# Eight gather slots in place of nine, and the page table loaded at the start of the last stage

## The reference

```python
hp = rmsnorm(xp, norm_mix)
b_g, c_g, x_in, q_lat, kv_lat, kr_raw, gate_c, gate_a = in_projection(hp, w_in)
attn = prompt_attention(...)          # causal, 8 heads; new tokens: sample_attention(...)
xp = xp + branch_merge(...)           # convolution branch and attention branch
xp = xp + peer(rmsnorm(xp, norm_ffn), ...)

def one_seq(args):                    # new tokens: keys come from pages of the cache
    pages, sqn, sqr, sckv, skr = args
    ckv_all = jnp.concatenate([pool_ckv[pages].reshape(-1, KV_LORA), sckv], axis=0)
    ...

def peer_block(h, w_peer_q, sub_keys, expert_u, expert_v):   # 8 heads, the best 16 of 16384 experts each
    ...
    a = jax.nn.gelu(jnp.einsum('thkd,td->thk', expert_u[eidx], h), approximate=False)
    return jnp.einsum('thk,thkd->td', g * a, expert_v[eidx])
```

## Time and profile before

| | us |
|---|---|
| median of 3 runs | 3808.12 (3807.24 to 3813.5) |
| the profiled execution: its own time | 3808.12 |
| its span in the profile | 3806.3 |
| first and last gather issued at | 639.9 and 3780.8 |
| PE, DVE, ACT, POOL busy | 3145.2, 2626.9, 1359.3, 1102.3 |
| DMA moved | 1289.23 MB, of it 1107.36 MB by the gathers |

### The profile page before, as it was taken

How to read it: one execution, slowest core, us unless ns; L and a number is a source line. 1 busy time by engine, 2 the same in 40 slices (tenths; PEclk the granted TensorE clock), 3 DMA queues, 4 the chain that set the end, 5 groups by cost and what they waited for, 6 DMA issues and landing times.

```text
span 3806.3 us, 35282 instructions
## 1 busy us (share of the span) xinstructions
PE 3145.2 (83%) x10224; PEld 1773.7 (47%) x10224; DVE 2626.9 (69%) x5829; ACT 1359.3 (36%) x3982; POOL 1102.3 (29%) x1252
## 2 busy tenths in 40 slices
PE   6797898858899999467878898899488988888877
PEld 4433686524555555134444454445144544566421
DVE  1355114987677789877677867789777677756874
ACT  1222202338712233255563222343244444212333
POOL 0000001343333333333333333334233333322342
PEclk9898699978899999788889999999699989766999
DMA  2112255999999998799999999999799899999999
GB/s 91 38 37 64 76 154 188 403 366 396 389 415 418 405 373 344 280 403 403 398 415 420 419 419 420 410 407 403 289 417 390 342 395 386 385 392 419 409 387 381
DMA packets 234016, 1289.23 MB, mean 339 GB/s; under 512 B 45467, under 2 KB 59867, under 8 KB 98340
## 3 DMA queue, kind: packets, MB, share of 16 engines
q0 software_dynamic: 152064, 1107.36, 71.6%
q1 hardware_dynamic: 80036, 175.28, 13.1%
q10 hardware_dynamic: 1728, 4.39, 0.3%
HBM read 1273.53 MB, written 13.40 MB: 338 GB/s over the span
## 4 chain that ended last, share of the span: by engine, by line
PE 30%; DMA 27%; DVE 21%; ACT 6%; issue 5%; POOL 2%; SPq 0%; DVEq 0%; POOLq 0%; ACTq 0%
DMA tl_uv<-in_uv,tl_idx 24%; PE tl_y L926 9%; DVE tl_uv L1501 7%; PE tl_f L1175 7%; DVE tl_acc L1482 4%; PE tl_f L1155 3%; PE tl_f L1203 2%; PE tl_f L1186 2%; PE tl_f L987 2%; PE tl_f L1099 1%; POOL tl_uv L857 1%; DMA w_tail<-in_w_merge 1%; PE tl_f L1051 1%; DMA w_tail<-in_w_conv 1%; DVE tl_eq L1601 1%
## 5 line engine op out<-in xcount | busy, mean ns | idle before, releaser
L1501 DVE CUSTOM_DVE_ANT_0 tl_uv<-tl_uv,tl_h 128x1024 f32<-128x1024 f32 x1056 | 1269.5, 1216 | 471.0 <-DMA tl_uv<-in_uv,tl_idx 460.6
L857 POOL DMA_INDIRECT tl_uv<-in_uv,tl_idx x1056 | 1043.8, 988 | 1770.8 <-PE tl_y L926 1071.5
L926 PE MATMUL tl_y<-tl_uv,tl_diag 128*128 128x512 f32 (+1 forms) x2428 | 1285.7, 672 | 292.9 <-ACT tl_diag L1222 292.2
L926 PEld LDWEIGHTS tl_y<-tl_uv,tl_diag 128*128 128x128 f32 (+1 forms) x2428 | 479.3, 209 | 931.5 <-issue 466.4
L1250 ACT ACTIVATE tl_ge<-tl_a 128x1 f32<-128x1 f32 x1056 | 210.1, 199 | 1230.8 <-DVE tl_a L1501 1229.0
L1482 DVE SCALAR_TENSOR_TENSOR tl_acc<-tl_uv,tl_w,tl_acc 128x1024 f32<-128x1024 f32 x441 | 565.1, 1281 | 65.2 <-ACT tl_w L1234 65.0
L1234 ACT ACTIVATE tl_w<-tl_ge,tl_weight 128x1 f32<-128x1 f32 x1024 | 301.5, 294 | 33.4
L1175 PE MATMUL tl_f<-H,w_tail 128*128 128x384 f32 (+2 forms) x1024 | 271.6, 424 | 13.5 <-DMA w_tail<-in_w_merge 11.9
L869 POOL TENSOR_TENSOR tl_cand<-tl_tv 128x48 f32<-128x48 f32 (+5 forms) x128 | 39.5, 337 | 823.5 <-DVE tl_ti L1533 623.5
L1203 PE MATMUL tl_f<-H,w_tail 128*128 128x384 f32 (+2 forms) x1024 | 262.6, 412 | 6.4 <-DVE H L1803 6.4
L1222 ACT ACTIVATE tl_diag<-K,tl_w 128x128 f32<-128x128 f32 (+1 forms) x607 | 241.2, 397 | 38.7 <-PE tl_y L926 19.6
(11 more groups left out here) (227 smaller groups left out, 3084.7 us busy)
## 6 DMA issues: line engine op xcount, KB each, us to landing
w_tail<-in_w_merge SPq DMA_DIRECT2D x96, 512.0 KB, 7.9
w_tail<-in_w_peer SPq DMA_DIRECT2D x64, 576.0 KB, 7.9
w_tail<-in_w_conv SPq DMA_DIRECT2D x48, 512.0 KB, 7.9
tl_uv<-in_uv,tl_idx POOLq DMA_INDIRECT x1056, 12.5
w_tail<-in_w_mix SPq DMA_DIRECT2D x32, 512.0 KB, 7.9
X<-in_cache SPq DMA_DIRECT2D x48, 128.0 KB
X<-in_x SPq DMA_DIRECT2D x8, 536.0 KB, 6.7
o_y<-tl_acc ACTq DMA_DIRECT2D x8, 512.0 KB, 6.2
```

The costliest lines, as they stand in the source:

```text
L857: pool.indirect_dma_start(UV[:, u % RING, :], None, d["uv"], bass.IndirectOffsetOnAxis(ap=which, axis=0)).then_inc(landed[u % RING], 16)
L926: mm = pe.matmul(Y[0:m, half * 512:(half + 1) * 512], DG[:, (pe_count[u] - 1) % DIAGS, 0:m], UV[:, u % RING, D + half * 512:D + (half + 1) ...
L1501: dve.tensor_tensor_reduce(UV[:, u % RING, 0:D], UV[:, u % RING, 0:D], HP[:], 1.0, 0.0, ALU.mult, ALU.add, A[:, t % 2, i:i + 1]).then_inc( ...
```

## The change

The ring has 8 slots in place of 9. That frees 8192 bytes of each partition. The page table moves from the overlaid region to a place of its own (256 bytes), and its load moves from `decode_loads` to the start of `tail_stage`. The wait for it (`tbl_in`) stays where it was, before the first page. The block that stands for the overlaid region gets 16 numbers (64 bytes) more. In the built program `tl_uv` begins at byte 136160 of a partition, 136096 before, and the tensors behind the ring come 8128 bytes lower, or 7872 bytes behind the page table.

```diff
-RING, WRING, DIAGS = 9, 3, 4
+RING, WRING, DIAGS = 8, 3, 4
...
-            PTB = sb("pages", [1, NSEQ * NPG], I32, c=decoding)
...
-        sb("shared", [P, (2 * CT + KD) * NMAX + 48])
+        sb("shared", [P, (2 * CT + KD) * NMAX + 64])
...
         ACC = sb("acc", [P, D])
+        PTB = sb("pages", [1, NSEQ * NPG], I32)
...
                 sp.dma_start(KRS[:], d["s_kr"]).then_inc(dec_in, 16)
-                sp.dma_start(PTB[:], d["pages"]).then_inc(tbl_in, 16)
                 sp.wait_ge(tbl_in, 16)
...
             sp.dma_start(STATE[:], d["state"]).then_inc(conv_in, 16)
+            sp.dma_start(PTB[:], d["pages"]).then_inc(tbl_in, 16)
```

## The result

| | before | after |
|---|---|---|
| median, us | 3810.81 (3807.24 to 3813.53, 4 runs) | 3855.88 (3852.59 to 3856.81, 4 runs) |
| the profiled execution: its own time | 3808.12 | 3849.86 |
| mean granted TensorE clock in it, as a share of 2.4 GHz (the lower level, 1.2, is 0.5) | 0.884 | 0.874 |

The two medians are 45 us apart. The ratio, estimated with further runs of the changed kernel, is 1.0108, with a 95% interval of [1.0092, 1.0125]: about 41 us slower. Measured once more in a later session it was 1.0101 [1.0082, 1.0120], 39 us. The forecast was 3826 us, +17.6, and its range ended at 3847, +39. The direction was right and the size was not.

What follows compares the result with a forecast made beforehand. It took the DMA engines' time at work (ceiling 420 GB/s, 2.50 us a gather) and time run dry as the bound. Slot 25.7, table -8.4, its load at the start +0.3: +17.6 on 3808.1, so 3826 us, range 3811 to 3847.

Steps and rivals of the forecast that it cites:

- The slot before and at the entry: Up to and with the entry of decode, the lost slot costs 10.0 + 7.5 + 2.5 = 20.0 us.
- the price of a dry stretch: Where DMA engines run dry, they do so one gather earlier and restart at the same release: 2.50 us; four before decode, 10.0.
- one new dry stretch in each: In three stretches before decode with fastest landings under 7.9 us, one newly dry stretch each: 7.5 us, between 0 and 20.
- The +2.5 us for the entry itself: At the entry of decode the ring fills one gather sooner and one less stands ready after it: +2.5 us.
- The slot behind the entry: Ten dry stretches behind the entry of decode, 2.5 us each, weighted 0.23 by DVE's waits for data: 5.7 us, between 0 and 25.
- Addresses: The ring 64 bytes higher and the tensors behind it lower, with the same engines, shapes and steps: 0.
- The table's load: At the entry of decode, page-number reads and page loads start 8.4 us earlier: -8.4 us, -8.1 with +0.3 at the start.
- A ninth of the ring: Rival: in stretches held by slots each unit takes 9/8 of its time, the upper ends hold: +49.4, 3857.5 us; chance 0.18.
- The table brings little: Rival: the last page loads land among gathers, so 2.4 us are gained in place of 8.4: 3832 us; chance 0.08.
- Eight are enough: Rival: dry stretches are made up for later, the slot costs nothing, the table's gain is left: 3800.0 us; chance 0.06.
- the two nearly cancel: Rival: only the four dry stretches and the entry pay for the slot, 12.5 - 8.1 = +4.4: 3812.5 us; chance 0.14.
- three signs of being wrong: Stretch up to 2700 us takes no longer, PE's wait for pages stays above 30 us, or full windows fall below 415 GB/s.

Runs made afterwards that it cites:

- ring8_only: Before with eight ring slots in place of nine, table's load and shared block as before: ratio 1.0084 [1.0066, 1.0103] to before.
- hold8_all: Before with nine slots at their places, but each gather waits for the release of the unit eight before it, whole span: ratio 1.0096 to before.
- shift_only: Before with the shared block 64 bytes larger, so the ring and all behind it lie 64 bytes higher: ratio 1.0021, again 1.0017, to before.
- hold8_early: Before with nine slots, but gathers below unit 720 (through the entry of decode) wait for the release of the unit eight before: ratio 1.0069 to before.
- ring8_table_first: The changed kernel without the 64 bytes more in the shared block (eight slots, table loaded at the start): ratio 1.0084 [1.0064, 1.0105] to before.
- ring7: The changed kernel with seven ring slots: ratio 1.0270 [1.0256, 1.0284] to before, 3918.7 us.

## Why the prediction was wrong

The sum of parts as measured: the slot 32 to 37 us (ring8_only, hold8_all), the place 6 to 8 (shift_only twice), the table -5.7 with eight slots (from the trace). That is 32 to 39, against the measured 39 to 41. The forecast had 25.7, 0 and -8.1. So of the miss of some 22 us about 9 are the slot's, 7 the place's, 3 the table's, and the rest is within the intervals.

*The slot before and at the entry: 20.0 forecast, 26 [18, 35] measured.* The failed step is the price of a dry stretch, that the DMA engines run dry one gather earlier "and start again at the same release: 2.50 us more", together with "I count one new dry stretch in each". The release does not stay where it was. In the second tile DVE waits 24 us longer for gathers, PE 10.5 us longer for DVE, and PE's products take 5 us more at a lower granted clock, so the slots come back later: at 1140.5 us in place of 1134.0 in the stretch that was followed above. The stretches at 1030 and 1443 us grew by 1 to 2 us and the one at 1595 not at all, less than the price. New ones opened at three places of the second tile alone and cost 3.0 to 4.8 us each. That tile is 16 us longer, and the sum had at most four prices in it, 10 us.

I took one gather for each of three minima, and allowed eight at most. The medians of 9.9 and 9.2 said that half of the gathers there had fewer than two others ahead. In before's trace 50 of the gathers issued up to 2700 us land within the 7.9 us of my test, 20 of them before 1450 us. That the price is convex (34, then 63 us) agrees: each slot taken uncovers gathers which the last one still covered.

The +2.5 us for the entry itself isn't seen there. The first gather behind it goes out 30.5 us after the load of `tl_kr` in before, and 27.9, 29.2 and 28.4 us after it in ring8_only, hold8_early and hold8_all: the ring of eight shortened the entry, since the table's load was through sooner. So the 26 us arise ahead of the entry.

The sum's lower end for the slot, 2.5 us, also leaves out the four dry stretches, for which no lower bound was given; with them it is 12.5.

*The slot behind the entry: 5.7 forecast, 10 [4, 16] measured.* The weight of 0.23 was mis-sized, though its interval holds the forecast. DVE's wait for data is a poor gauge. In the changed kernel it is 18.3 us for 151 products in the same window (compare), 3 us more, while the time grew by 10:

```profile
L1501 DVE CUSTOM_DVE_ANT_0 tl_uv<-tl_uv,tl_h x151: 1197/1212/1223, 2899.8 to 3349.6; 128x1024 f32<-128x1024 f32 x151
...
  DMA tl_uv<-in_uv,tl_idx: 18.3, 17
```

*Addresses: 0 forecast, 6 to 8 us measured.* This step failed as a whole: a term was put at nothing. "The same engines, shapes and steps" left out that the gathers' rate depends on where the ring begins, and the ceiling that the whole sum leant on was one of this place. I divided by 420 GB/s and never asked why it was 420. The rule of the Trainium skill that fits stands on the same page, DMA: Bandwidth & Descriptors, that the prediction drew on for other things.

*The table's load: -8.1 forecast, -8.4 [-13, -3] measured alone.* The mechanism and the size were right for nine slots. With eight, the removed wait had already shrunk from 8.4 us (2726.88 to 2735.3) to 5.7 (2757.28 to 2763.0, where the first read of ring8_only starts), so its removal was worth 5.7; PE's wait for the pages says the same, 30.0 us in ring8_only and 24.5 in ring8_table_first. I priced each edit against before and added, where one edit had made the other smaller: an error of 2.7 us. How much of the 5.7 reaches the end is not shown: ring8_only and ring8_table_first have the same ratio, and with intervals of 0.2% each way that can't tell 0 from 5.7.

*The load at the start, +0.3*, is too small to be told.

*The rivals.* "A ninth of the ring", 3857.5, has the time nearest to the result, but by three causes together and not by its own: the price of the slot is 34 us and not its 57.5. "The table brings little" was right in part, by another way than it said: the page loads did not land late, PE waits 24.6 us. "Eight are enough" and "the two nearly cancel" fell with the slot's 32 to 37 us. None of the three signs of being wrong appeared: the stretch up to 2700 us takes longer, PE's wait is 24.6 us and the full windows are at 419. They tested whether the terms were there, not their size.

*What stays open.* Some 4 us between the middles of the sum of parts (36) and of the whole (40) lie within the intervals. How much of the slot's price passes through PE's clock is not separated from the waits. The mean granted clock fell with the depth, from 0.879 over before's 23 runs to 0.875 in ring8_only's and 0.869 in ring7's, and PE is busy for 3180.5 us in the changed kernel's trace against 3145.2. In the second tile this part is 5 of 16 us; a run that holds the clock and shortens the ring is missing. The chain from DVE's waits to PE's was followed in the second tile alone.

## What to carry to other kernels

Ask of a measured ceiling what it depends on: here the begin of the gathers' buffer, a multiple of 256 or not, was worth 0.6 to 0.8% of the kernel, and a change of some buffer's size moves every buffer behind it. Price the loss of a queue's depth by how many transfers have little ahead of them (the median landing against the least) and by who waits behind each late one, not by one transfer's time for each stretch that is already dry. And price edits together where one changes the queue that the other one waits in.

## What the runs showed of the hardware

- Gathers of 8 KB rows into SBUF ran at 426 GB/s where the buffer begins at a multiple of 256 bytes (136192, 136448), and at 418 to 420 where it begins at a multiple of 32, 64 or 128 only (136096, 136160, 136128, 136320).
- A load of 64 numbers from SP, issued with four gathers of 1 MiB still to land, could be read 8.4 us later, and 5.7 us later with three still to land. The read began within 0.5 us of the last of these landings: a small load pays for the large ones that are on the DMA engines.
- After a wait of 4.8 us PE took 13.5 us for 32 products which took 10.6 after a wait of 1.3 us, at a granted clock of 0.80 in place of 1.00. A wait of PE cost more than its own length.
- The time of one program moved with the mean granted TensorE clock. In one session before ran 23 times: the seven shortest, 3804 to 3812 us, had a mean clock of 0.880 to 0.888, the nine longest, 3819 to 3823 us, one of 0.875 to 0.879. Which of the two moves the other is not shown. The profiled execution of before (0.884) is like the former and that of the changed kernel (0.874) is not. So two traces can differ by 10 us with no change in the kernel, and the sizes above are taken from ratios of many runs.
